# x is transposed once; the first shift and scale are made with features on partitions

## What is computed

```python
cs = jax.nn.silu(c)
for layer in range(DEPTH):
    mod = (cs @ mod_w[layer] + mod_b[layer]).reshape(bsz, N_SUB, 3, D_MODEL)
    x = adaln_sublayer(x, mod[:, 0], lambda u: 0.5 * swiglu(u, ffn_w_gate[layer, 0], ...), ...)
    ...

def adaln_sublayer(x, m, f, ln_g, ln_b):
    shift, scale, gate = m[:, None, 0], m[:, None, 1], m[:, None, 2]
    y = f(x * (1 + scale) + shift)
    return layer_norm(DEEPNORM_ALPHA * x + (1 + gate) * y, ln_g, ln_b)
```

## Time and profile before

| | us |
|---|---|
| median of 3 runs | 2396.93 (2388.88 to 2405.09) |
| the profiled execution, its time | 2387.18 |
| its span, first to last instruction | 2385.3 |
| mean granted TensorE clock | 0.956 |
| TensorE busy | 2166.9 |
| VectorE, ScalarE, GpSimd busy | 1374.0, 997.9, 266.4 |

### The profile page before, as it was taken

One profiled execution on the slowest core, in us unless ns is written; L12 is line 12 of the kernel. 1 busy time (PEld: TensorE's weight loads), 2 busy tenths in 40 slices (PEclk: granted clock), 3 DMA queues, 4 the chain that ended last, 5 costly groups with the idle time before them and its releaser, 6 DMA issues.

```text
span 2385.3 us, 30476 instructions
## 1 busy us (share of the span) xinstructions
PE 2166.9 (91%) x12408; PEld 1775.8 (74%) x12408; DVE 1374.0 (58%) x1986; ACT 997.9 (42%) x1563; POOL 266.4 (11%) x298
## 2 busy tenths in 40 slices
PE   5999888988999999968999978889899988897999
PEld 3777678866778777746767866767799876776997
DVE  3544657846545755645755455656576455665663
ACT  1443353324444444335433434334455344344552
POOL 0000200012000200111210021321000112310000
PEclk9999889988999999989999989999899999998999
DMA  9686473415866876563656653235566552354664
GB/s 307 215 269 230 126 195 107 141 63 185 274 228 202 263 259 207 189 200 124 189 180 200 200 124 105 79 106 166 144 187 193 161 137 71 100 166 115 183 183 138
DMA packets 374491, 412.11 MB, mean 173 GB/s; under 512 B 27511, under 2 KB 319563, under 8 KB 374352
## 3 DMA queue, kind: packets, MB, share of 16 engines
q1 hardware_dynamic: 367216, 388.37, 52.7%
q0 software_dynamic: 7136, 21.81, 2.9%
HBM read 407.49 MB, written 2.62 MB: 172 GB/s over the span
## 4 chain that ended last, share of the span: by engine, by line
PE 73%; DVE 9%; DMA 5%; issue 4%; POOL 4%; ACT 4%; SPq 0%; POOLq 0%; DVEq 0%; ACTq 0%
PE ps L169 70%; PE ps L172 3%; POOL arena L178 3%; DVE arena L178 2%; DVE wlo L178 2%; DMA arena<-in_mod_w 1%; DVE arena L190 1%; ACT whi L175 1%; ACT arena L175 1%; DMA raw<-in_ffn_w_up 1%; POOL small L178 1%; DVE tmp L190 1%; DVE tmp L178 1%; DMA raw<-in_w_up 1%; DMA modrel<-in_mod_b 1%
## 5 line engine op out<-in xcount | busy, mean ns | idle before, releaser
L178 DVE TENSOR_TENSOR wlo<-raw,whi 128x1024 fp32r<-128x1024 f32 (+1 forms) x592 | 720.7, 1237 | 474.2 <-ACT whi L175 471.8
L175 ACT ACTIVATE whi<-raw 128x1024 fp32r<-128x1024 f32 (+1 forms) x592 | 607.2, 1049 | 341.2 <-DMA raw<-in_w_up 87.6
L169 PE MATMUL ps<-whi,uh 128*128 128x512 f32 (+1 forms) x1298 | 539.1, 416 | 56.0 <-ACT arena L175 19.6
L169 PE MATMUL ps<-wlo,uh 128*128 128x512 f32 (+1 forms) x1298 | 516.5, 398 | 0.0
L169 PE MATMUL ps<-whi,ul 128*128 128x512 f32 (+1 forms) x1298 | 417.0, 396 | 0.0
L169 PE MATMUL ps<-whi,arena_r 128*128 128x512 f32 x1184 | 371.9, 392 | 3.5 <-DVE arena_r L178 2.5
L169 PEld LDWEIGHTS ps<-whi,uh 128*128 128x128 f32 x1298 | 251.7, 194 | 145.4 <-issue 41.3
L169 PE MATMUL ps<-uh,whi 128*128 128x256 f32 x984 | 286.0, 291 | 16.9 <-DVE arena L190 13.4
L169 PEld LDWEIGHTS ps<-whi,ul 128*128 128x128 f32 x1298 | 249.0, 193 | 58.2
L169 PEld LDWEIGHTS ps<-wlo,uh 128*128 128x128 f32 x1298 | 252.2, 194 | 51.4 <-issue 0.7
L169 PE MATMUL ps<-ul,whi 128*128 128x256 f32 x984 | 281.7, 286 | 0.0
(11 more groups left out here) (211 smaller groups left out, 1840.9 us busy)
## 6 DMA issues: line engine op xcount, KB each, us to landing
arena<-in_mod_w SPq DMA_DIRECT2D x60, 1024.0 KB, 6.9
raw<-in_w_in SPq DMA_DIRECT2D x90, 512.0 KB, 3.6
raw<-in_ffn_w_gate SPq DMA_DIRECT2D x176, 256.0 KB, 4.0
raw<-in_ffn_w_up SPq DMA_DIRECT2D x176, 256.0 KB, 4.7
raw<-in_ffn_w_down SPq DMA_DIRECT2D x88, 512.0 KB, 4.2
raw<-in_w_up SPq DMA_DIRECT2D x88, 512.0 KB, 3.9
raw<-in_w_down SPq DMA_DIRECT2D x44, 512.0 KB, 3.5
raw<-in_hyb_w_in SPq DMA_DIRECT2D x32, 512.0 KB, 3.9
```

The source lines that it names most:

```text
L169: return Nothing() if self.raw is None else self.raw.matmul(out, l, r, start=start, stop=stop)
L175: return Nothing() if self.raw is None else self.raw.activation(out, src, func, **kw)
L178: return Nothing() if self.raw is None else self.raw.tensor_tensor(out, a, b, op)
```

## The change

Features go on partitions from the start. x is loaded ahead of the groups and transposed once (16 transposes, banks 0 to 3), and ScalarE copies it to `tmp` (`x_turned`). The sum over bands becomes, per quarter, four products with one column of `rows4`, whose left operand is a slice of 128 columns of the partial sums: the result has features on partitions, one column for each half of shift and scale. The biases are loaded as 16 rows of 128 and transposed together with c. u is then x_turned times a factor plus a term, each a column: ScalarE makes the rounded u in one Identity activation per 128 features, VectorE makes the full u with one two-operator instruction per 128 features and subtracts. The constants are ordered anew (`rows4` and `freq` now stand behind `ident`); SP loads the first 272 columns at the start and the rest behind quarter 1. In the loop chunk 0 of q - 1 comes ahead of the groups of q, chunk 1 ahead of the sum, chunk 2 behind it. ScalarE and VectorE take two units ahead of u and one behind it.

In the diff a removed body of which only the first and the last line stand is printed whole above.

```diff
@@ -43,6 +43,8 @@
     same = j // 64 == i // 64
     parts = {
         "ident": np.eye(P),
+        "rows4": np.tile((np.arange(P) % 32 == 0)[:, None], (1, P)),
+        "freq": np.tile(np.float32(10000.0) ** (-np.arange(16, dtype=np.float32) / np.float32(16)), (P, 1)),
         "ones": np.ones((P, P)),
         "tri": same & (j <= i),
         "same": same,
@@ -72,6 +70,7 @@
     CONST_AT[_k] = (CONST_N, _v.shape[1])
     CONST_N += _v.shape[1]
 CON = CONST_AT["hot"][0]
+CON_FIRST = CONST_AT["ones"][0]
 
 class Two:
@@ -650,10 +649,16 @@
 
+def first_rows(M):
+
+    return out_u(M)[0:3 * KD, 0:P]
+
 def sp_setup(sp, M):
-    A = M.A
-    sp.dma(M.tmp[0:KD, 0, 0:P], A["c"].rearrange("a (k p) -> (a k) p", p=P)).then_inc(*sp.dv("ld_c"))
-    sp.dma(M.con[:, :], A["consts"][:, 0:CON]).then_inc(*sp.dv("ld_con"))
+    A, rows = M.A, first_rows(M)
+    sp.dma(rows[0:KD, :], A["c"].rearrange("a (k p) -> (a k) p", p=P)).then_inc(*sp.dv("ld_c"))
+    sp.dma(M.con[:, 0:CON_FIRST], A["consts"][:, 0:CON_FIRST]).then_inc(*sp.dv("ld_con"))
+    sp.dma(rows[KD:3 * KD, :], A["mod_b"][0, 0:2 * D].rearrange("(i p) -> i p", p=P)).then_inc(*sp.dv("ld_modb1"))
 
 def pool_setup(pool, M):
@@ -662,21 +667,26 @@
 
 def pe_setup(pe, M):
-    pe.wait_ge(*pe.on("ld_con"))
-    pe.wait_ge(*pe.on("ld_c"))
-    tr(pe, M, fill(pe, M, 4, ("silu_c",))[:, 0:KD], M.tmp[0:KD, 0, 0:P]).then_inc(*pe.ev("c_tr"))
+    pe.each(pe.on("ld_con"), pe.on("ld_c"), pe.on("ld_modb1"))
+    tr(pe, M, fill(pe, M, 4, ("silu_c",), ("first_b",))[:, 0:3 * KD], first_rows(M)).then_inc(*pe.ev("c_tr"))
 
 def act_setup(act, M):
-    act.wait_ge(*act.on("ld_con"))
     act.wait_ge(*act.on("c_tr"))
     act.activation(M.cst, M.bank(4)[:, 0:KD], ACT.Silu).then_inc(*act.ev("silu_c"))
 
+def first_bias(M):
+
+    return [M.col(x, 2 * KD).rearrange("p (a k) -> p a k", a=2) for x in ("first_b", "first_s")]
+
 def dve_setup(dve, M):
-    dve.wait_ge(*dve.on("ld_con"))
+    b, _ = first_bias(M)
     dve.wait_ge(*dve.on("silu_c"))
     dve.copy(M.csb[:, :, :], M.cst.unsqueeze(2).broadcast_to([P, KD, 32])).then_inc(*dve.ev("csb"))
+    dve.copy(b[:, 0, :], M.bank(4)[:, KD:2 * KD])
+    dve.ts(b[:, 1, :], M.bank(4)[:, 2 * KD:3 * KD], 1.0, None, ALU.add).then_inc(*dve.ev("first_b"))
 
 def positions_views(M):
@@ -1105,26 +1115,33 @@
 
-def open_bias(M, part):
-    return M.tmp[:, 1, :] if part else M.modb
+
+def x_turned(M):
+    return M.tmp[:, :, :].rearrange("p t d -> p (t d)").rearrange("p (k s) -> p k s", s=S)
+
+def open_u(M, q):
+
+    return out_u(M)[:, q % 2 * 512:q % 2 * 512 + 512].rearrange("p (k s) -> p k s", s=S)
 
 def both_sums(M):
     return M.modrel[:, D:D + 512]
 
-def open_u(M, q):
...
-
 def pe_open(pe, M):
-    units = {}
+    pe.wait_ge(*pe.on("ld_x"))
+    for j in range(4):
+        bank = fill(pe, M, j, ("x_turned", j))
+        for k in range(2):
+            for t in range(T):
+                at, f = k * S + t * P, (2 * j + k) * P
+                last = tr(pe, M, bank[:, at:at + P], M.x[:, t, f:f + P])
+        last.then_inc(*pe.ev("x_tr", j))
     for q in range(5):
+        if q:
+            pe_open_chunk(pe, M, 0, q - 1)
         if q < 4:
             bank = fill(pe, M, 7, ("mod_ms", 4 + q))
             pe.wait_ge(*pe.on("csb"))
@@ -1136,22 +1153,17 @@
                     last = pe.matmul(bank[j:j + 32, 256 * part:256 * part + 256], M.csb[:, k, :],
                                      mod_set(M, gi)[1][:, k, :], k < 4, k >= 4)
                 last.then_inc(*pe.ev("mod_mv", gi))
-        for c in range(OPEN):
...
-                last.then_inc(*pe.ev("u_tr", -1, q))
+        if q:
+            pe_open_chunk(pe, M, 1, q - 1)
+        if q < 4:
+            bank = fill(pe, M, 7, ("mod_fix", 4 + q))
+            pe.wait_ge(*pe.on("mod_ms", 4 + q))
+            for i in range(4):
+                last = pe.matmul(bank[:, i:i + 1], both_sums(M)[:, i * P:i * P + P], M.c("rows4")[:, 0:1], True, True)
+            last.then_inc(*pe.ev("mod_sum", 4 + q))
+        if q:
+            pe_open_chunk(pe, M, 2, q - 1)
+    pe.wait_ge(*pe.on("ld_con2"))
 
 def pe_open_chunk(pe, M, c, q):
@@ -1164,9 +1176,9 @@
         b = course(0).bank[2 * c + t]
         out = M.bank(b) if q else fill(pe, M, b, ("h", 0, 2 * c + t))
         toks = slice(t * P, (t + 1) * P)
-        pe.wait_ge(*pe.on("u_hi", -1, q))
         pe.wait_ge(*pe.on("lo", uid))
         for i in range(2):
+            pe.wait_ge(*pe.on("u_hi", -1, 2 * q + i))
             pe.matmul(out, M.uT.hi[:, 2 * q + i, toks], v.hi[:, i, :], q == 0 and i == 0, False)
             pe.matmul(out, M.uT.hi[:, 2 * q + i, toks], v.lo[:, i, :], False, False)
         pe.wait_ge(*pe.on("u_lo", -1, q))
@@ -1178,71 +1190,65 @@
             last.then_inc(*pe.ev("up0", 0, c))
 
-def open_turned(M, q):
-    return M.uT[:, 2 * q:2 * q + 2, :], M.bank(6).rearrange("p (k s) -> p k s", s=S)
-
-
 def act_open(act, M):
-    for q in range(5):
-        if q < 4:
-            if q:
-                act.wait_ge(*act.on("mod_sum", 3 + q))
-            act.wait_ge(*act.on("mod_mv", 4 + q))
-            act.activation(both_sums(M), M.bank(7), ACT.Copy).then_inc(*act.ev("mod_ms", 4 + q))
+    for j in range(4):
+        act.wait_ge(*act.on("x_tr", j))
+        act.activation(x_turned(M)[:, 2 * j:2 * j + 2, :], M.bank(j).rearrange("p (k s) -> p k s", s=S),
+                       ACT.Copy).then_inc(*act.ev("x_turned", j))
+    _, sv = first_bias(M)
+    for q in range(4):
         if q:
-            act_unit(act, M, OPEN)
-        if q < 4:
-            dst, src = open_turned(M, q)
-            act.wait_ge(*act.on("u_tr", -1, q))
-            act.activation(dst.hi, src, ACT.Copy).then_inc(*act.ev("u_hi", -1, q))
+            act.wait_ge(*act.on("mod_sum", 3 + q))
+        act.wait_ge(*act.on("mod_mv", 4 + q))
+        act.activation(both_sums(M), M.bank(7), ACT.Copy).then_inc(*act.ev("mod_ms", 4 + q))
+        act_unit(act, M, OPEN - 1)
+        act.wait_ge(*act.on("mod_fix", 4 + q))
+        act.wait_ge(*act.on("x_turned", q))
+        for k in range(2 * q, 2 * q + 2):
+            act.activation(M.uT.hi[:, k, :], x_turned(M)[:, k, :], ACT.Identity, scale=sv[:, 1, k:k + 1],
+                           bias=sv[:, 0, k:k + 1]).then_inc(*act.ev("u_hi", -1, k))
+        act_unit(act, M, 1)
         if q == 1:
             act_positions(act, M)
 
 def dve_open(dve, M):
-    dve.wait_ge(*dve.on("ld_x"))
...
-            dve.tt(dst.lo, src, dst.hi.bitcast(F32), ALU.subtract).then_inc(*dve.ev("u_lo", -1, q))
+    b, sv = first_bias(M)
+    for q in range(4):
+        ks, u = slice(2 * q, 2 * q + 2), open_u(M, q)
+        dve_unit(dve, M, OPEN - 1)
+        dve.wait_ge(*dve.on("first_b"))
+        dve.wait_ge(*dve.on("mod_sum", 4 + q))
+        dve.tt(sv[:, :, ks], M.bank(7)[:, 0:4].rearrange("p (a k) -> p a k", a=2), b[:, :, ks], ALU.add).then_inc(
+            *dve.ev("mod_fix", 4 + q))
+        dve.wait_ge(*dve.on("mod_fix", 4 + q))
+        dve.wait_ge(*dve.on("x_turned", q))
+        if q > 1:
+            dve.wait_ge(*dve.on("u_lo", -1, q - 2))
+        for k in range(2):
+            i = 2 * q + k
+            last = dve.ts(u[:, k, :], x_turned(M)[:, i, :], sv[:, 1, i:i + 1], sv[:, 0, i:i + 1], ALU.mult, ALU.add)
+        last.then_inc(*dve.step("ln_v"))
+        dve.wait_ge(*dve.prev("ln_v"))
+        dve.wait_ge(*dve.on("u_hi", -1, 2 * q + 1))
+        dve.tt(M.uT.lo[:, ks, :], u, M.uT.hi[:, ks, :].bitcast(F32), ALU.subtract).then_inc(*dve.ev("u_lo", -1, q))
+        dve_unit(dve, M, 1)
+    dve.wait_ge(*dve.on("ld_con2"))
 
 def sp_open(sp, M):
-    for q in range(5):
...
-            sp_units(sp, M, OPEN)
+    sp.dma(M.x[:, :, :], M.A["x"].rearrange("b (t p) d -> p (b t) d", p=P)).then_inc(*sp.dv("ld_x"))
+    for q in range(4):
+        sp_mod(sp, M, q)
+        sp_mod(sp, M, 4 + q)
+        sp_units(sp, M, OPEN)
+        if q == 1:
+            sp.dma(M.con[:, CON_FIRST:CON], M.A["consts"][:, CON_FIRST:CON]).then_inc(*sp.dv("ld_con2"))
     sp_units(sp, M, 8)
 
 def pool_open(pool, M):
     pool_positions(pool, M)
-    pool_bias(pool, M, 0)
-    pool.dma(open_bias(M, 1), M.A["mod_b"][0, D:2 * D].partition_broadcast(P)).then_inc(*pool.dv("ld_modb1"))
     pool_bias(pool, M, 2)
```

More of the change, by code:

```diff
@@ L56, in constant_parts @@
     parts["cmpadd"] = np.where(seen, 0.0, NEG).reshape(P, -1)
-    parts["rows4"] = np.tile((np.arange(P) % 32 == 0)[:, None], (1, P))
-    half = 16
-    freq = np.float32(10000.0) ** (-np.arange(half, dtype=np.float32) / np.float32(half))
-    parts["freq"] = np.tile(freq, (P, 1))
     hot = np.zeros((P, 384))
@@ L1202, in dve_open @@
 def dve_open(dve, M):
-    dve.wait_ge(*dve.on("ld_x"))
-    for q in range(5):
-        if q:
-            dve_unit(dve, M, OPEN - 1)
-        if q < 4:
-            sl, u = quarter(q), open_u(M, q)
-            dve.wait_ge(*dve.on("mod_sum", 4 + q))
-            dve.each(dve.on("ld_modb", 0), dve.on("ld_modb1"))
-            for part in range(2):
```

(27 more changed lines are left out.)

17 lines of the change are left out of this document (removed).

## The result

| | before | after |
|---|---|---|
| median of 6 runs, us | 2392.9 (2388.0 to 2405.8) | 2366.9 (2358.9 to 2378.3) |
| ratio of the two, 95% interval | | 0.990 (0.987 to 0.993) |
| the profiled execution: time, span | 2387.2, 2385.3 | 2368.7, 2366.8 |
| its mean granted clock | 0.956 | 0.956 |
| chunk 0 of the four quarters starts at | 30.5, 47.2, 64.0, 75.9 | 22.0, 35.4, 47.2, 58.6 |

The kernel is about 1% faster: 26 us by these medians, 17 to 31 by the interval. The last row is the mark on which the prediction was made. It came 17.3 us earlier, where 19.7 were predicted. Two more profiled executions of the changed kernel have it at 58.8 and 58.9, so a mark of one execution is good to about 0.3 us. The profiled executions differ by 18.5.

A forecast was written before the change was run, and what follows sets the result against it. The opening was taken as bound by a cross-engine chain, with the load second, and the rest by matmuls. The last quarter's chunk 0 moves from 75.9 to 56.2: 2396.9 - 19.7 = 2377 us, range 2363 to 2389.

The forecast's parts named there:

- The bound and the chain: In the opening TensorE has room and waits on a cross-engine chain; it lost 9.9 us to weights' residues in six places.
- The start, 21.1: Chunk 0 of quarter 0 would start on TensorE at 21.1 us, against 30.5 before.
- landing = 4.7 + MB / 0.350: Landing time in us from the MB queued up to a load, calibrated on group 4's landing at 16.45 before.
- Chunk 0 of quarter 0, 4.15: The first quarter's chunk 0 on TensorE would take 4.15 us as before, from 21.1 to 25.3.
- The factors, 0.6: Each quarter's four one-column products with rows4 would take 0.6 us together on TensorE's path.
- Group 6, a wait of 0.9: After chunk 0 of quarter 1 ends at 36.5 us, TensorE would wait for group 6, landing at 37.4.
- Edits costed at nothing: x's transposes (2.4 to 4.4 us), u's margins, SP's unit 8 and POOL's later loads would be hidden, cost 0.
- A: Rival for the opening: the summed schedule holds, last quarter's chunk 0 at 56.2 against 75.9, 19.7 us gained; chance 0.60.
- B: Rival for the opening: quarters paced by the load and at the low clock, 11.7 us gained; chance 0.17.
- C: Rival for the opening: TensorE alone sets the pace, last quarter's chunk 0 at 53.6, 22.3 us gained; chance 0.15.
- D: Rival behind the opening: the load paces stage 0 and the gain is given back, about 5 us gained; chance 0.05.
- E: Rival for the opening: slower, as u now hangs on units as well as groups; gives 2420 us; chance 0.03.

The follow-up runs named there:

- order_alone: The kernel before with x loaded first and the new order of the loops, but its old mathematics; median 2386.8 us, ratio 0.9957.
- math_alone: The changed kernel with the old order of the loops, x still loaded first; median 2379.5 us, ratio 0.9941.
- busy_gap: The changed kernel plus four 128x448 products that nothing reads, in TensorE's idle time ahead of quarter 0's chunk 0; one run, 2361.3 us.

## Why the prediction was right, and where it was off

*The bound and the chain.* Right. TensorE's waits for residues went, and order_alone and math_alone show that the order did it.

*The start, 21.1; it was 22.0.* **The landing times were mis-sized.** The line "landing = 4.7 + MB / 0.350" was fitted at one point, with 0.83 MB of constants in front. With 0.14 MB in front the queues moved 67 GB/s up to 5.2 us and not 174, so the line gives too early a time. Group 4's matmuls began at 15.8, not 14.5. Of these 1.3 us 0.9 came back by a second miss: the matmuls took 1.07 us and not 1.94. They stand behind the transposes, and in before and in order_alone, which have none there, both groups took 1.93 or 1.94. On the way to u two small things were added. The second unit landed 0.3 late for ScalarE, of which 0.1 reached VectorE, and from the start of u's first slice to TensorE's start it was 0.74 and not 0.45. That is 0.9 us late in all.

*Chunk 0 of quarter 0, 4.15.* It took 4.96, at a granted clock of 0.50 up to 24 us. I had taken the length from before, where the wait ahead of it was also there; how much of it falls in the low stretch differs: 4.2 us in before, and 4.8, 5.0, 5.3, 5.4 and 5.4 in the five executions of the changed kernel's order that wait for 3.3 us; 3.3 where the clock stayed up.

*The factors, 0.6.* They took 0.81 from their first start to the next chunk's, and each of the four is recorded as two, so the four fast transposes (0.6) were too low a guess: 0.2 in each of three quarters. VectorE's operations with two columns took 0.41 and not 0.35. The small add took 0.16, for 0.2.

*Group 6, a wait of 0.9.* It was 0.24, since chunk 0 had already made TensorE late; group 7 was not waited for. But group 6 itself landed at 39.57 and not 37.4. These 2.2 us are more than the slow start explains: the queues had moved 12.30 MB by then, and my sum has 11.46 up to the end of this group. So loads issued behind it had taken part of the rate, more than at the point of the fit (4.48 MB moved for 4.11), and a line that takes all loads in strict order has no term for that.

*The rest of the sum.* Each chunk took 2.9 us and not 2.8, 0.7 over eight of them, and the groups needed no 0.3 ahead of their 1.93 in quarters 0 and 2, 0.8 less; the two cancel. Together the terms are + 0.9 (start), + 0.8 (quarter 0), + 0.6 (quarter 1) and + 0.1 (quarter 2): 2.4 us, from 56.2 to 58.6.

*Edits costed at nothing.* x's transposes (3.36 us, 9.8 to 13.2) lay ahead of the groups' landing, as said. SP's unit 8 and POOL's loads cost nothing; POOL's first waited until 53.7. u's margin against chunk 0 of quarter 2 was 1.6 us by my sum, and u was there at 45.6, needed at 47.2: it was 1.6.

*The rivals.* A was right in kind. Of B one part holds: a wait of 3.3 us ahead of chunk 0 cost clock once (busy_gap: 1.7 us), but the load did not pace the quarters. The Trainium skill (TensorE: Matmul & The Clock Gate, "HAM oscillation — how this bites in real kernels") tells of a kernel whose waits for loads are longer than the work between them, and whose clock falls at each of them. Here the quarters have no waits to speak of and a clock of 1.00 from 28 us on, so its condition was not met. But the prediction says for B that the trace shows no wait of 1 us in which the clock fell, and that is a misreading: the trace of before has such waits behind the opening. TensorE waited 1.16 us ahead of 309.0 us and was busy from there on, and the clock, 0.95 from 308 to 310 us, was 0.50 from 310 to 312. From 513 to 516 us it fell too (0.77), behind waits of 0.38 and 0.55 us. So short waits did not make B as unlikely as its chance has it; in the changed kernel there were none behind 28 us to try it. C, TensorE alone, describes 22 us onward, though its start was too early. D and E did not happen: the rest of the span is the same.

*The total.* 2377 was 10 us above the median. 4 of these are the base: 2396.9 was the median of the first three runs of before, 2392.9 that of the six beside the changed kernel. The other 6 are 26.0 between the medians in place of 19.7, though the mark gave only 17.3: the total came out better than forecast while the step that was forecast came out worse, and that they partly make up for each other is luck. "What follows is the same program, so the shift is the gain" was right for the profiled executions (17.3 of 18.5) and short by some 6 us for the mean of many.

## What to carry to other kernels

Where a chain crosses engines, look for what can be made small before it spreads (here a sum turned so that its features lie on partitions, four columns in place of 512) and move the engines' order with it: either alone gave less than half of what both gave. When TensorE and the load end within a microsecond of each other, a gain on one turns into a wait for the other, so price both before touching one. And don't carry a landing time that was fitted at one point over to a queue with another start: here the first 5 us moved 67 GB/s or 174, by the size of the first load.
